# Attention in one encoder layer: the second unit's exponential on the common maximum, and another order of ScalarE's instructions

## What is computed

```python
def block_attention(q, k, v):
    ...
    scale = 1.0 / math.sqrt(dh)

    def one_block(qi):
        s = jnp.einsum('bqkgd,bskd->bkgqs', qi, k).astype(jnp.float32) * scale
        p = jax.nn.softmax(s, axis=-1).astype(v.dtype)
        return jnp.einsum('bkgqs,bskd->bqkgd', p, v)

    out = lax.map(one_block, qb)
```

## Time and profile before

| | |
|---|---|
| median of three runs | 4936.14 us |
| the three runs | 4936.14, 4944.38, 4927.88 us |
| the profiled execution, its own time | 4955.78 us |
| its span (first to last instruction) | 4954.1 us |
| TensorE busy | 4263.9 us, 86% of the span |
| VectorE busy | 3031.0 us, 61% |
| ScalarE busy | 2036.9 us, 41% |
| GpSimd busy | 1150.6 us, 23% |
| mean granted clock of TensorE | 0.931 |

### The profile page before, as it was taken

One profiled execution on the slowest core, in us unless ns is written; L12 is line 12 of the kernel. 1 busy time (PEld: TensorE's weight loads), 2 busy tenths in 40 slices (PEclk: granted clock), 3 DMA queues, 4 the chain that ended last, 5 costly groups with the idle time before them and its releaser, 6 DMA issues. The chain is left out here.

```text
span 4954.1 us, 142712 instructions
## 1 busy us (share of the span) xinstructions
PE 4263.9 (86%) x61165; PEld 3942.2 (80%) x61166; DVE 3031.0 (61%) x5716; ACT 2036.9 (41%) x3616; POOL 1150.6 (23%) x951
## 2 busy tenths in 40 slices
PE   6979999986888867777777777992799999999998
PEld 5868888865888866667776775772799999999998
DVE  6879999954888874444444445767545444444443
ACT  4568888854555531111111112220344444444443
POOL 4533333321333320100100212320121211211110
PEclk9989999977999979998999988995899999999999
DMA  9910000004333331122112115650465655655654
GB/s 168 184 46 22 24 21 22 24 27 126 129 128 131 131 136 55 55 62 60 55 55 67 55 56 158 203 157 3 158 182 166 178 177 170 183 168 175 177 170 109
DMA packets 519591, 542.01 MB, mean 109 GB/s; under 512 B 75200, under 2 KB 456384, under 8 KB 519104
## 3 DMA queue, kind: packets, MB, share of 16 engines
q1 hardware_dynamic: 411840, 425.00, 27.2%
q10 hardware_dynamic: 92480, 62.93, 5.7%
q0 software_dynamic: 14784, 46.57, 4.5%
HBM read 377.99 MB, written 156.43 MB: 108 GB/s over the span
## 5 line engine op out<-in xcount | busy, mean ns | idle before, releaser
L2287 DVE TENSOR_TENSOR g_wlo<-g_raw,g_whi 128x2048 fp32r<-128x2048 f32 x192 | 439.3, 2288 | 115.4 <-ACT g_whi L2249 115.4
L2249 ACT ACTIVATE g_whi<-g_raw 128x2048 fp32r<-128x2048 f32 x192 | 366.4, 1909 | 145.2 <-DMA g_raw<-expert_w_gate 145.2
L2358 PE MATMUL g_pD<-g_whi,g_hh 128*128 128x256 f32 x1536 | 417.6, 285 | 2.5 <-ACT g_o L2276 2.4
L2358 PE MATMUL g_pD<-g_wlo,g_hh 128*128 128x256 f32 x1536 | 408.4, 279 | 0.0
L517 POOL TENSOR_SCALAR saprob<-saprob,sarate 128x1024 f32<-128x1024 f32 x256 | 283.7, 1121 | 458.6 <-DVE sarate L597 458.6
L1107 PE MATMUL c_pP<-c_xh,c_whi 128*128 128x258 f32 x1120 | 335.8, 300 | 46.8 <-DMA c_gup<-g_lora_up 28.3
L540 ACT ACTIVATE saph<-sapT 128x512 fp32r<-128x512 f32 x512 | 291.5, 596 | 125.8 <-PE sapT L636 125.6
L1372 DVE TENSOR_TENSOR d_pm<-d_pP,d_fixed 128x128 f32<-128x128 f32 x400 | 114.3, 289 | 365.1 <-PE d_pP L1429 364.6
L1259 POOL TENSOR_TENSOR d_kr<-d_kr,d_fixed 128x512 f32<-128x512 f32 x80 | 103.1, 1293 | 1009.2 <-ACT d_kr L1293 1009.0
L581 DVE TENSOR_TENSOR sapl<-sapT,saph 128x512 fp32r<-128x512 f32 x512 | 329.1, 685 | 2.5 <-ACT saph L540 2.5
L571 DVE TENSOR_REDUCE sanm<-sapS 128x1 f32<-128x1024 f32 x256 | 312.7, 1221 | 26.1 <-PE sapS L624 16.3
(11 more groups left out here) (361 smaller groups left out, 14236.7 us busy)
## 6 DMA issues: line engine op xcount, KB each, us to landing
g_raw<-expert_w_gate SPq DMA_DIRECT2D x64, 1024.0 KB, 5.6
g_raw<-expert_w_up SPq DMA_DIRECT2D x64, 1024.0 KB, 5.5
g_raw<-expert_w_down SPq DMA_DIRECT2D x64, 1024.0 KB, 5.2
ops<-c_ops SPq DMA_DIRECT2D x40, 1024.0 KB, 4.0
d_bd<-ops SPq DMA_DIRECT2D x80, 512.0 KB, 3.9
c_xh<-xT_hi SPq DMA_DIRECT2D x10, 1032.0 KB, 5.6
c_xl<-xT_lo SPq DMA_DIRECT2D x10, 1032.0 KB, 8.6
x_in<-x SPq DMA_DIRECT2D x20, 512.0 KB, 8.1
```

What stands on the lines that cost most here:

```text
L2249: act.activation(w_hi[:, Q % NBUF, :, :], raw[:, Q % NRAW, :, :], ACT.Copy).then_inc(s["g_hi"], 1)
L2287: dve.tensor_tensor(w_lo[:, Q % NBUF, :, :], raw[:, Q % NRAW, :, :], w_hi[:, Q % NBUF, :, :].bitcast(F32), ALU.subtract).then_inc(s["g_lo" ...
L2358: mm = pe.matmul(pD[k][:, 0:WB], x[:, d, k * P:(k + 1) * P], w[:, b, d, :], start=(d == 0 and i == 0), stop=(d == DC - 1 and i == len(part ...
```

## The change

Three things, all in `attention`:

1. The exponential of the second unit subtracts the common minimum `nmin` in place of its own; it waits for `common`. The first unit's still uses its own minimum. So only the first unit has a share, one column, and the second unit's is 1.
2. The divisor takes two VectorE instructions (share times the first sum plus the second sum, then the reciprocal) in place of four; GpSimd multiplies by the rate and, for the first unit, by the share, in one instruction as before.
3. In ScalarE's queue a unit's exponential stands between its two copies of high parts, where it stood behind both. `shares` has one more wait, for GpSimd's first multiplication of head h-2, since the share is now read there.

With one unit and one block (the short sequence) the code gives the same instructions in the same order as before.

```diff
@@ -512,7 +512,8 @@
                     for u in range(NU):
                         keys = slice(u * UW, (u + 1) * UW)
-                        pool.tensor_scalar(prob[:, h % 4, keys], prob[:, h % 4, keys], rate[:, h % 2, u:u + 1], 1.0, ALU.mult, ALU.mult).then_inc(s["norm"], 1)
+                        to_common = share[:, h % 2:h % 2 + 1] if u < NU - 1 else 1.0
+                        pool.tensor_scalar(prob[:, h % 4, keys], prob[:, h % 4, keys], rate[:, h % 2:h % 2 + 1], to_common, ALU.mult, ALU.mult).then_inc(s["norm"], 1)
...
             def exps(t, h, u):
                 if live(t):
-                    act.wait_ge(s["nm"], NU * head(t, h) + u + 1)
-                    act.activation(prob[:, h % 4, u * UW:(u + 1) * UW], pS[u][:].rearrange("p k n -> p (k n)"), ACT.Exp, bias=nm[:, h % 2, u:u + 1],
+                    if u == 0:
+                        act.wait_ge(s["nm"], NU * head(t, h) + 1)
+                    else:
+                        act.wait_ge(s["nmin"], head(t, h) + 1)
+                    act.activation(prob[:, h % 4, u * UW:(u + 1) * UW], pS[u][:].rearrange("p k n -> p (k n)"), ACT.Exp,
+                                   bias=nm[:, h % 2, 0:1] if u == 0 else nmin[:, h % 2:h % 2 + 1],
                                    scale=-1.0, accum_out=den[:, h % 2, u:u + 1]).then_inc(s["exp"], 1)
 
             def shares(t, h):
 
                 if live(t):
                     act.wait_ge(s["nmin"], head(t, h) + 1)
-                    act.activation(share[:, h % 2, :], nm[:, h % 2, :], ACT.Exp, bias=nmin[:, h % 2:h % 2 + 1], scale=-1.0).then_inc(s["share"], 1)
+                    tb, hb = back(t, h, 2)
+                    if live(tb):
+                        act.wait_ge(s["norm"], NU * head(tb, hb) + 1)
+                    act.activation(share[:, h % 2:h % 2 + 1], nm[:, h % 2, 0:1], ACT.Exp, bias=nmin[:, h % 2:h % 2 + 1], scale=-1.0).then_inc(s["share"], 1)
...
             def step(t, h):
                 turning = back(t, h, 2)
                 for u in range(NU):
-                    for k in range(NB):
+                    high(*turning, NB * u)
+                    exps(t, h, u)
+                    for k in range(1, NB):
                         high(*turning, NB * u + k)
-                    exps(t, h, u)
                     if u == 0:
                         evacuate(*back(t, h, 6))
...
                     dve.wait_ge(s["share"], head(t, h) + 1)
-                    dve.tensor_tensor(part[:, h % 2, :], den[:, h % 2, :], share[:, h % 2, :], ALU.mult).then_inc(s["part"], 1)
-                    dve.wait_ge(s["part"], head(t, h) + 1)
-                    dve.tensor_reduce(dsum[:, h % 2:h % 2 + 1], part[:, h % 2, :], AX.X, ALU.add).then_inc(s["ds"], 1)
+                    k = slice(h % 2, h % 2 + 1)
+                    dve.scalar_tensor_tensor(out=dsum[:, k], in0=den[:, h % 2, 0:1], scalar=share[:, k], in1=den[:, h % 2, 1:2],
+                                             op0=ALU.mult, op1=ALU.add).then_inc(s["ds"], 1)
                     dve.wait_ge(s["ds"], head(t, h) + 1)
-                    dve.reciprocal(rden[:, h % 2:h % 2 + 1], dsum[:, h % 2:h % 2 + 1]).then_inc(s["rd"], 1)
-                    dve.wait_ge(s["rd"], head(t, h) + 1)
-                    dve.tensor_scalar(rate[:, h % 2, :], share[:, h % 2, :], rden[:, h % 2:h % 2 + 1], None, ALU.mult).then_inc(s["rate"], 1)
+                    dve.reciprocal(rate[:, k], dsum[:, k]).then_inc(s["rate"], 1)
```

More of the change, by code:

```diff
@@ L449, in attention @@
         nmin = sb(name + "nmin", [P, 2])
-        share = sb(name + "share", [P, 2, NU])
-        part = sb(name + "part", [P, 2, NU])
+        share = sb(name + "share", [P, 2])
         prob = sb(name + "prob", [P, 4, nk])
@@ L454, in attention @@
         dsum = sb(name + "dsum", [P, 2])
-        rden = sb(name + "rden", [P, 2])
-        rate = sb(name + "rate", [P, 2, NU])
+        rate = sb(name + "rate", [P, 2])
         ph = sb(name + "ph", [P, 2, n_tiles, 2, P], F32R)
@@ L462, in attention @@
         pO = [ps(f"{name}pO{k}") for k in range(2)]
-        s = sems("id q0 q1 score nm nmin exp share part ds rd rate norm tr hi lo pv osb st0 st1 seen", name + "_")
+        s = sems("id q0 q1 score nm nmin exp share ds rate norm tr hi lo pv osb st0 st1 seen", name + "_")
         block = ctx.enter_context(nc.Block())
@@ L587, in total @@
                     if NU == 1:
-                        dve.reciprocal(rate[:, h % 2, :], den[:, h % 2, :]).then_inc(s["rate"], 1)
+                        dve.reciprocal(rate[:, h % 2:h % 2 + 1], den[:, h % 2, :]).then_inc(s["rate"], 1)
                         return
                     dve.wait_ge(s["share"], head(t, h) + 1)
-                    dve.tensor_tensor(part[:, h % 2, :], den[:, h % 2, :], share[:, h % 2, :], ALU.mult).then_inc(s["part"], 1)
-                    dve.wait_ge(s["part"], head(t, h) + 1)
-                    dve.tensor_reduce(dsum[:, h % 2:h % 2 + 1], part[:, h % 2, :], AX.X, ALU.add).then_inc(s["ds"], 1)
+                    k = slice(h % 2, h % 2 + 1)
+                    dve.scalar_tensor_tensor(out=dsum[:, k], in0=den[:, h % 2, 0:1], scalar=share[:, k], in1=den[:, h % 2, 1:2],
+                                             op0=ALU.mult, op1=ALU.add).then_inc(s["ds"], 1)
                     dve.wait_ge(s["ds"], head(t, h) + 1)
-                    dve.reciprocal(rden[:, h % 2:h % 2 + 1], dsum[:, h % 2:h % 2 + 1]).then_inc(s["rd"], 1)
-                    dve.wait_ge(s["rd"], head(t, h) + 1)
-                    dve.tensor_scalar(rate[:, h % 2, :], share[:, h % 2, :], rden[:, h % 2:h % 2 + 1], None, ALU.mult).then_inc(s["rate"], 1)
+                    dve.reciprocal(rate[:, k], dsum[:, k]).then_inc(s["rate"], 1)
             def step(t, h):
```

## The result

The changed kernel takes 5139.74 us (median of four runs, 5121.10 to 5147.19), the kernel before 4932.01 us (four runs, 4925.44 to 4944.38): ratio 1.0416, 95% interval 1.0388 to 1.0443. The forecast was 5135. The medians differ by 208 us, and the long attention stage is longer by 199.

A forecast was written before the change was run, and what follows sets the result against it. The prediction took a VectorE-TensorE loop of 5.76 us a head as the bound, replaced by a ScalarE-VectorE chain of 7.34; 126 x (7.34 - 5.76) = +199 us on 4936 gave 5135 us, range 5105 to 5180.

The forecast's parts named there:

- The loop of before: Long attention stage before the change: VectorE and TensorE close a loop of 5.77 us a head; ScalarE is not in it.
- The chain of the new order: Long stage: reduction, exponential, copy, subtraction, next reduction become the loop, period at least 7.34 us a head, where it was 5.76.
- The step list: Start-to-start steps 1.26, 1.09, 0.63, 0.60 us make the first half 3.58; the second, with the common minimum's 0.19, 3.76.
- Nothing from the arithmetic under the new order: The denominator's two fewer VectorE operations save 0.34 us a head, all inside VectorE's wait for the second copy: worth nothing.
- 126 steps times the difference: Long stage, steps 2 to 127: 126 x (7.34 - 5.76) = +199 us.
- The clock: TensorE in the long stage keeps the full granted clock, 1.00, although idle 1.8 of 7.34 us a head.
- the rival with the low clock: TensorE's clock falls to 0.50 in the long stage: 5410 us if for half of the heads, +748 for all; chance 5%.
- the one with ScalarE off the loop: Long stage: copy 1 comes in time despite the exponential, TensorE's 5.55 us rules, 27 us faster, 4909 us; chance 4%.
- the one with a single half: Long stage: the first half's exponential does not hold copy 1; period 6.48 us, +91 us, 5027 us; chance 4%.
- nearness to the fill: Full clock taken because TensorE's expected 76% busy is nearest the stage's fill, 299.6 to 312.4 us, 79% at clock 1.00.
- the term of TensorE's own work: Long stage: TensorE could do a head in 5.77 - 0.22 = 5.55 us and no less.
- what TensorE has to spare under the new order: Long stage: TensorE needs 2.60 us from a subtraction to the next scores' end, against 3.0 and 3.2 until VectorE wants them.

The follow-up runs named there:

- the first experiment: Changed kernel with ScalarE's old order (copy, copy, exponential), the rest of the change kept: 4907.11 us, ratio 0.9873 to the kernel before, period 5.453 us.
- the order alone: Kernel before with only ScalarE's order changed to copy, exponential, copy: 5147.94 us, ratio 1.0347 to the kernel before, period 7.161 us.
- the last runs: Kernel before, changed kernel and changed kernel with ScalarE's old order, each rerun unchanged on one chip: 4967.95, 5170.08 and 4913.25 us.
- the arithmetic alone: Changed kernel with ScalarE's old order, against the kernel before: ratio 0.9873, and 0.9908 (4913.25 us) when run again.

## Why the prediction was right

*The loop of before* held. The prediction says that the waits show only ScalarE and GpSimd waiting; the same view has a third row, which is this very loop, TensorE's weight loads held by the subtractions twice a head:

```profile
PEld sapT L636 <- DVE sapl L581: 55.7, 230, 0.3
```

With half the exponential the loop kept its 5.77 us, so ScalarE is not in it; with less arithmetic on VectorE it fell to TensorE's 5.45, and that row was gone (the first experiment).

*The chain of the new order* held. The step list gave 3.58 + 3.76 = 7.34 us; measured are 3.58 + 3.77 = 7.35. The four steps are in the trace one by one (1.26, 1.09, 0.63, 0.60 foretold; 1.25, 1.10, 0.62, 0.61 found), and VectorE's waits were 0.78 and 1.12 us (0.8 and 1.1 foretold). Halving the exponential, doubling the copies behind it and undoing one half each moved the period by what the list says, the last together with TensorE's 3.3 us from subtraction to reduction.

*Nothing from the arithmetic under the new order*: shown by the order alone. Its long stage is 908 us, that of the whole change 931; the two differ by the common minimum's step (0.19 x 126 = 24 us), which makes the whole change the slower one, and the 0.34 us of VectorE work saved do not show.

*126 steps times the difference*: 199 us, measured 198.7 and 198.6 in the stage, in two pairs of profiles. That is the figure that bears the theory out. That the median came within 5 us of the forecast is in part luck: the medians differ by 208 and 213, the profiled spans by 179 and 199, and the 9 to 14 us beyond the stage were not traced. They are no larger than the spread of the kernel before alone (4938 to 4974 us on the chip of the last runs).

*The clock*: 1.00 through the stage with TensorE busy 80% of the time, so the rival with the low clock did not come about, nor did the one with ScalarE off the loop or the one with a single half. The ground given for the full clock was weak, though: the short stage had a larger busy share (75.8 of 89 us) than the fill (10.13 of 12.8) and the lower clock, so nearness to the fill in that share decided nothing, and this part came out without having been shown. What the Trainium skill tells of one bf16 kernel in TensorE: Matmul & The Clock Gate, section "A second HAM failure mode: psum-queue depth-cycling", that small idles between groups send the clock back and forth, no trace of the long stage here shows; it stayed up even with 754 of 1040 us busy (the exponential ahead of both copies).

*Mis-sized*: the term of TensorE's own work, 5.55 us, is 5.45. I had taken out the stall in the transposes (0.22) but not the smaller ones in the steps from scores to transposes: 0.93 us in the earlier trace rows (702.91 to 703.84) and 0.97 from its last row to the transposes below, where the trace of the first experiment has 0.91. The arithmetic alone is therefore worth 39 us in the stage, not 27. This did not enter the forecast, since under the new order it is hidden.

```profile
706.63 1.25 PE L636 MATMUL sapT<-saidentf,saprob 128*128 128x128 f32 x8
```

Also mis-sized, in part for the same reason, is what TensorE has to spare under the new order. In the changed kernel:

```profile
703.40 0.66 PE L641 MATMUL sapT<-saidentf,saprob 128*128 128x128 f32 x4 [0.82 <-DVE sapl L588]
...
704.82 1.09 PE L629 MATMUL sapS<-KT,saq 128*128 128x512 f32 x4
...
706.98 0.66 PE L641 MATMUL sapT<-saidentf,saprob 128*128 128x128 f32 x4 [0.64 <-DVE sapl L588]
```

The subtraction ends at 703.34 (702.65 + 0.69), the scores at 705.91, 2.57 us later, and VectorE takes them at 706.84, 3.50 us later, where the prediction has 2.60 against 3.0. So 0.9 us are to spare and not 0.4, and TensorE is idle 1.47 us a head, not 1.8. Neither changes the sum.

The kernel with the arithmetic alone beats both: 0.9873 and 0.9908 of the kernel before in two sets of runs.

## What to carry to other kernels

An instruction moved within an in-order queue brings all its waits to everything behind it. Before moving it, write down what waits for the instruction behind and what that in turn holds up; if the list comes back to the moved instruction's own releaser, the whole chain becomes the period, and its steps can be read from any place of the old trace where each of them waited. Work saved on an engine is worth only what the loop through it leaves to the next one: here 39 us by itself, nothing beside the new chain.

## What was not expected of the hardware

The short attention stage has two lengths with the same instructions. In the kernel before, TensorE's granted clock stayed at 0.50 (1.2 GHz) in it with 75.8 of 89 us busy. In the first profile of the arithmetic alone it rose to 1.00 (2.4 GHz) after a low start and stayed there, with 38.3 of 60 us busy:

```profile
1010.00:1020.00 10.00, 5.38 (x14) 3.26 (x14) 3.27 (x8) 3.63 (x9) 2.07 (x3) 0.50 0.04 10
1030.00:1090.00 60.00, 38.32 (x236) 30.32 (x234) 34.58 (x72) 33.39 (x84) 16.60 (x24) 1.00 0.16 48
```

The stage then takes 83 instead of 106 us. Of twelve profiles three had it so; in the others the clock rose late (93, 100, 104 or 105 us) or not by the last score matmul (106). The recurrence varies more: it takes 1128 to 1164 us from its first to its last matmul into d_pX in the twelve profiles, with the same instructions in all of them, and no cause was found. A difference of some 20 to 35 us between two kernels of this program can be these alone, so the gain or loss of a stage is better read from that stage's own first and last row.
